# A two-block forward pass in one kernel: new SBUF addresses for the operands of the matmuls

## The reference

```python
def first_block(x, ...):
    for i in range(2):
        if i == 0:   # gated spatial mixing and a 31-tap causal convolution
            z = rms_norm(x, g) @ even_w_in + b            # 1024 -> 2048
            x = x + concat([ya, yb]) @ even_w_out         # 1024 -> 1024
        else:        # dilated attention, 16 heads of 64
            q, k, v = rms_norm(x, g) @ odd_w_qkv          # 1024 -> 3072
            x = x + attention(rotary(q), rotary(k), v) @ odd_w_o
        u = causal_dwconv(rms_norm(x, g) @ w_up, ...)     # 1024 -> 2 * 2816, 3 taps
        x = x + (silu(gate) * val) @ w_down               # 2816 -> 1024
    return rms_norm(x, final_norm_g)

def second_block(x, ...):
    for l in range(2):
        proj = h @ w_in[l]                                # about 2700 columns
        mixed = concat([nsa_mixer(...), gla_mixer(...), pool_mixer(...)])
        h = layer_norm(alpha * h + mixed @ w_out[l])      # 1024 -> 1024
        ff = square(relu(h @ w_up[l])) @ w_down[l]        # 1024 -> 4096 -> 1024
        h = layer_norm(alpha * h + ff)
```

## Time and profile before

| | |
|---|---|
| median of three runs | 2616.25 us (2608.53 to 2621.46) |
| the profiled execution's own time | 2612.8 us |
| its span, first to last instruction | 2611.1 us |
| granted TensorE clock, mean | 0.980 |
| TensorE matmul busy | 2479.2 us, 95% |
| VectorE, ScalarE busy | 1417.0 us, 1086.7 us |
| matmul records | 11,814 |

### The profile page before, as it was taken

How to read it: one execution, slowest core, us unless ns; L and a number is a source line. 1 busy time by engine, 2 the same in 40 slices (tenths; PEclk the granted TensorE clock), 3 DMA queues, 4 the chain that set the end, 5 groups by cost and what they waited for, 6 DMA issues and landing times.

```text
span 2611.1 us, 33416 instructions
## 1 busy us (share of the span) xinstructions
PE 2479.2 (95%) x11814; PEld 1937.2 (74%) x11814; DVE 1417.0 (54%) x2298; ACT 1086.7 (42%) x1649; POOL 51.7 (2%) x64
## 2 busy tenths in 40 slices
PE   8989999999998999998998989999989889899997
PEld 6667888877776788886766668888857666788885
DVE  5876777236763777724357664244263774533424
ACT  4535444237882544413445443133153553432322
POOL 0000000000000000000012000000000200000000
PEclk9999999999999999999999999999999999999999
DMA  4112333321222233323211123333322112222321
GB/s 169 59 48 88 96 96 96 91 86 58 64 65 65 88 97 96 94 91 117 66 49 41 49 65 97 92 93 97 97 86 66 36 38 73 69 96 92 96 97 65
DMA packets 57422, 210.38 MB, mean 81 GB/s; under 512 B 6478, under 2 KB 6880, under 8 KB 56960
## 3 DMA queue, kind: packets, MB, share of 16 engines
q1 hardware_dynamic: 56736, 204.51, 25.0%
q0 software_dynamic: 608, 4.81, 0.5%
HBM read 207.20 MB, written 2.10 MB: 80 GB/s over the span
## 4 chain that ended last, share of the span: by engine, by line
PE 82%; DVE 8%; ACT 6%; issue 2%; DVEq 1%; DMA 0%; SPq 0%; ACTq 0%
PE PS L1071 14%; PE PS L1073 13%; PE PS L1072 13%; PE PS L1087 10%; PE PS L1088 10%; PE PS L1089 10%; PE PS L1108 2%; ACT PT L710 1%; PE PS L1246 1%; ACT RT L722 1%; ACT PB L704 1%; DVE RSTD L1648 1%; DVE WL L1625 1%; DVE PB L1876 1%; PE PS L1099 1%
## 5 line engine op out<-in xcount | busy, mean ns | idle before, releaser
L1625 DVE TENSOR_TENSOR WL<-RAW,WH 128x1024 fp32r<-128x1024 f32 x376 | 462.4, 1230 | 666.9 <-ACT WH L545 666.3
L545 ACT ACTIVATE WH<-RAW 128x1024 fp32r<-128x1024 f32 x376 | 397.4, 1057 | 834.9 <-PE PS L1089 576.5
L1071 PE MATMUL PS<-HH,WH 128*128 128x512 f32 x1792 | 713.1, 398 | 1.9 <-DVE WL L1625 1.9
L1073 PE MATMUL PS<-HH,WL 128*128 128x512 f32 x1792 | 699.6, 390 | 0.0
L1072 PE MATMUL PS<-HL,WH 128*128 128x512 f32 x1792 | 699.1, 390 | 0.0
L1071 PEld LDWEIGHTS PS<-HH,WH 128*128 128x128 f32 x1792 | 337.4, 188 | 77.2 <-issue 6.8
L1073 PEld LDWEIGHTS PS<-HH,WL 128*128 128x128 f32 x1792 | 337.0, 188 | 71.0
L1072 PEld LDWEIGHTS PS<-HL,WH 128*128 128x128 f32 x1792 | 337.6, 188 | 69.8 <-issue 3.3
L1089 PE MATMUL PS<-MH,WL 128*128 (+1 forms) x864 | 340.9, 395 | 0.0
L1088 PE MATMUL PS<-ML,WH 128*128 (+1 forms) x864 | 340.9, 395 | 0.0
L1087 PE MATMUL PS<-MH,WH 128*128 (+1 forms) x864 | 340.9, 395 | 0.0
(11 more groups left out here) (273 smaller groups left out, 2571.2 us busy)
## 6 DMA issues: line engine op xcount, KB each, us to landing
RAW<-wstream SPq DMA_DIRECT2D x376, 512.0 KB, 3.5
W<-cmp_w POOLq DMA_DIRECT2D x2, 2048.0 KB, 8.7
X<-xt SPq DMA_DIRECT2D x4, 512.0 KB, 6.5
out<-X SPq DMA_DIRECT2D x8, 256.0 KB, 2.2
TAB<-tables SPq DMA_DIRECT2D x1, 1871.5 KB, 12.6
WS<-spatial_w SPq DMA_DIRECT2D x1, 512.0 KB, 8.5
BS<-spatial_b SPq DMA_DIRECT2D x1, 256.0 KB, 8.9
PW<-pool_w POOLq DMA_DIRECT2D x2, 128.0 KB, 2.3
```

The costliest lines, as they stand in the source:

```text
L545: act.activation(WH[:, b, :], RAW[:, b, :], ACT.Copy).then_inc(w_hi, 1)
L1071: pe.matmul(PS[:, bank, :], WH[:, b, w], HH[:, k, :], start=(k == 0), stop=False)
L1073: last = pe.matmul(PS[:, bank, :], WL[:, b, w], HH[:, k, :], start=False, stop=(k == DC - 1))
L1625: dve.tensor_tensor(WL[:, b, :], RAW[:, b, :], WH[:, b, :].bitcast(F32), ALU.subtract).then_inc(w_lo, 1)
```

## The change

Only addresses change. `TAB` is placed first, then a filler, so that `X`, `HH`, `HL`, `RAW`, `WH` and `WL` start at a multiple of 2048 bytes. `VEC` moves behind them. The scopes `ffn`, `odd` and `ffn2` begin with a filler that brings their first tensor to a multiple of 2048, and `OH`, `OL` move ahead of the small tensors of `odd`. The fillers are never read or written.

```diff
+ROW_BYTES = 2048
+SMALL = 128
+TAB_FILL = (-SMALL - (TAB_COLS + 7) // 8 * 32) % ROW_BYTES // 4
+SCOPE_FILL = (-((VEC_COLS + 7) // 8 * 32) - 64) % ROW_BYTES // 4
...
+        TAB = sb("TAB", [P, TAB_COLS])
+        sb("FILL", [P, TAB_FILL])
         X = sb("X", [P, DC, T])
         HH = sb("HH", [P, DC, T], F32R)
         HL = sb("HL", [P, DC, T], F32R)
         RAW = sb("RAW", [P, 2, D])
         WH = sb("WH", [P, 2, D], F32R)
         WL = sb("WL", [P, 2, D], F32R)
-        VEC = sb("VEC", [P, VEC_COLS])
-        TAB = sb("TAB", [P, TAB_COLS])
         MU = sb("MU", [P, T])
         RSTD = sb("RSTD", [P, T])
         STD = sb("STD", [P, T])
+        VEC = sb("VEC", [P, VEC_COLS])
         WARM = sb("WARM", [P, len(NORM)])
...
         with ExitStack() as ffn:
+            sb("FILLF", [P, SCOPE_FILL], scope=ffn)
             NBF = sb("NBF", [P, DC, T], scope=ffn)
...
         with ExitStack() as odd:
+            sb("FILLO", [P, SCOPE_FILL], scope=odd)
             NBO = sb("NBO", [P, DC, T], scope=odd)
             COSR, SINR = NBO[:, 0, :], NBO[:, 1, :]
+            OH = sb("OH", [P, PAIRS, T], F32R, scope=odd)
+            OL = sb("OL", [P, PAIRS, T], F32R, scope=odd)
             QRAW = sb("QRAW", [P, T], scope=odd)
...
-            OH = sb("OH", [P, PAIRS, T], F32R, scope=odd)
-            OL = sb("OL", [P, PAIRS, T], F32R, scope=odd)
...
         with ExitStack() as ffn2:
+            sb("FILL2", [P, SCOPE_FILL], scope=ffn2)
             NB2 = sb("NB2", [P, DC, T], scope=ffn2)
```

## The result

The kernel after the change takes 2593.78 us (median of five runs, 2592.54 to 2597.57), the one before 2616.25 us (median of five, 2608.17 to 2621.46). The ratio is 0.9923, with a 95% interval from 0.9902 to 0.9944: a gain of 15 to 26 us. It is estimated from all executions; the two medians alone would give 0.9914. The forecast was 2596 us and a gain of 18.7.

The account below looks back on a forecast made before the run. TensorE's matmuls, busy 95% of the span, were taken to bound the kernel. Gains of 17.1 + 1.3 + 0.3 = 18.7 us, off 2612.8, gave 2594.1, stated as 2596 us for the median; range 2492 to 2622.

Parts of the forecast that it names:

- parts 1 and 2: add_rows matmuls on MH, ML, MH2, ML2 (1) and OH, OL (2) reach 226.7 ns: 17.1 and 1.3 us gained.
- rival C: Remainder 0 gives all streams 233.3 ns: HH and HL lose 40.8 us, time 2654 us; chance 0.09.
- Part 3: Matmuls on HH and HL, remainder 128 to 0: zero taken, bounds 67.4 us gained and 40.8 us lost.
- Part 4: Weights WH and WL, remainder 128 to 0: zero, since slices at four remainders already had an even pitch.
- Part 5: Score matmuls: QS, KS, KL go to 0, some 0.3 us gained; ZS goes from 320 to 544, zero.
- Parts 6 and 7: Plain float32 matmuls (6): zero, 1 us either way; VectorE (7): no difference from addresses, nothing new late.
- A: All fp32r streams reach 215.8 ns at multiples of 2048: 116.2 us, time 2497; chance 0.27, whole or in part.
- B: Place in the partition sets the pitch: MH, ML, OH, QS stay, 2613 us; chance 0.17 with other no-change cases.

Follow-up runs that it names:

- Run 5: Kernel after the change with MH and ML moved to remainder 128, MH2 and ML2 to 256, OH and OL to 384, weights at 0: 2601.46 us, executed once.
- run 3: Kernel after the change with everything from X on 64 bytes higher, weights and moving operands alike: ratio 0.994 to the kernel before.
- Run 2: Kernel after the change with only WH and WL moved up by 64 bytes: median 2649.73 us, ratio 1.0149 to the kernel before.
- run 10: Kernel after the change with MH and ML at remainder 16, MH2 and ML2 at 240, OH and OL at 48, weights at 0: 2615.30 us, executed once.
- runs 2 to 7: Kernel after the change with weights, moving operands or both shifted: ratios 1.0149, 0.994 to the kernel before, then 2608.31, 2601.46, 2610.71, 2630.20 us.

## Why the prediction was right, and where it was right for the wrong reason

**What bounds the kernel, and parts 1 and 2.** The size was right, and the gain is clear of no change as the prediction counts it, from 0.5% on. MH, ML, OH and OL went from 233.3 to 226.7 ns, and 2592 + 192 matmuls at 6.6 to 6.7 ns are 18.5 us; the ratio times 2616.25 gives 20 us, with 15 to 26 in the interval. The reason given, that 128 and 0 are multiples of 128 and the others not, was wrong. Run 5 has moving operands at a multiple of 128 and 233.3 ns, run 3 has them at 64 and 226.7. The rows could not tell "HH's address" from "the weights' address", since HH and HL had the weights' remainder. That the numbers agreed was luck: the change happened to give MH, ML, OH and OL a multiple of 128 and the weights' remainder at once. The right rule stood in the prediction, as the argument against rival C (HH, RAW, WH and WL "had one remainder in common before as well, and were the fast ones"), and was not made a rival of its own.

**Part 3.** HH and HL kept 226.7, as taken, because their distance to WH and WL stayed 0 by 256 bytes. Under my reason this rested on a guess; by the table of distances it follows.

**Part 4 was wrong in its argument.** It took the weights' start to be without effect since four slices of a tile, 512 bytes apart, had an even pitch. 512 is a multiple of 256, so they could show nothing. Run 2 moved the weights alone and cost 20 ns a triple, 2.3% against the layout after (1.0149 / 0.9923).

**Part 5 was wrong by its 0.3 us.** Scores read weights and moving operand from QS and KS or KL, or both from ZS, whose starts differ by multiples of 256 in either layout. KS and QS have 359 ns before and 358 after the earlier trace rows. It also said that ZS at 320 was at no multiple of 64; 320 is 5 x 64, and nothing hung on it.

**Parts 6 and 7 held.** Float32 matmuls keep 592 ns, VectorE 683 and 685.

**The rivals.** A (a floor of 215.8 at multiples of 2048) did not come: `project` has 226.8. B (the place in the partition) fell with the change itself, since MH at 133,120 is as fast as HH. C (HH gets slow) did not come here, but its price was real: run 2 showed 700.0 ns on HH and HL and a kernel slower than before by 1.5%. A change that puts the moving operands at multiples of 2048 and the weights 64 bytes past one ends there, for it is run 2.

The note on cachelines in the Trainium skill ("SBUF — State Buffer", section on Door 1) ties full bandwidth to consecutive accesses to one 16-byte line. By that alone every start at a multiple of 16 bytes would be alike. The trace disagrees: a shift of 16 bytes (run 10) costs 15 ns a triple.

**What stays open.** Why multiples of 256 are the good distances, why +64 costs 8 ns and -64 costs 20 (on OH and OL), and what the 13.4 ns above 213.3 are. The table is what the runs show; no mechanism behind it was shown. That weight reads and moving reads get in each other's way fits runs 2 to 7, but is an argument and no measurement.

## What to carry to other kernels

Where fp32r matmuls stand back to back, put the moving operands and all weight tiles (here WH and WL) at the same remainder by 256 bytes. The common remainders tried, 0, 64 and 128, did equally well. Measure the distance between starts in a stretch where TensorE never waits: 6.6 ns on 2784 matmuls were worth 18.5 us here, and TensorE's busy share was 95% before and after. When two tensors share a property in the only trace there is, say which of the two a rule rests on, and move one of them alone.

## What the runs showed of the hardware

- An fp32r matmul of 128 x 512, with its own weight load, has a pitch of 226.7 ns at the full granted clock at best, where moving operand and weights start a multiple of 256 bytes apart. At 32, 128, 192, 224 and 240 it has 233.3, at 16 it has 231.7. Float32 records stay at 592 ns of duration.
- Triples were seen at 680.0, 693.3 and 700.0 ns, but also at 688.4, 689.3, 695.0 and 696.0. In run 2 the mean pitch is 233.3, but single pitches are 230 to 236.
- At half the clock the distance costs nothing. In `add_rows` on HH and HL, in a stretch at half clock, 6 pitches are 2.56 us, 426.7 ns each, in run 2 (weights 64 off, 233.3 at the full clock) as after the change (226.7):

```profile
1494.79 0.63 PE L1098 MATMUL PS<-HH,WH 128*128 128x512 f32 x1
...
1497.35 0.47 PE L1098 MATMUL PS<-HH,WH 128*128 128x512 f32 x1
```

```profile
1470.72 0.63 PE L1099 MATMUL PS<-HH,WL 128*128 128x512 f32 x1
...
1473.28 0.63 PE L1099 MATMUL PS<-HH,WL 128*128 128x512 f32 x1
```

- Halving one or two of the three weight loads of a triple makes it longer: 689.3 and 688.4 ns instead of 680.0.
